# A small GpSimd memset behind each V gather, and a wait for it

## The reference, cut to what matters

```python
def expert_block(args):          # ht: 128 tokens x 1024, it: 128 x 128 indices, gt: 128 x 128 gates
    ht, it, gt = args
    ue = jnp.take(u, it, axis=0)                       # a row of u for each index
    act = jax.nn.gelu(jnp.einsum('tkd,td->tk', ue, ht), approximate=False)
    ve = jnp.take(v, it, axis=0)                       # a row of v for each index
    return jnp.einsum('tk,tkd->td', gt * act, ve)
```

## Time and profile before

| what | value |
|---|---|
| median of 3 runs | 1728.86 us |
| lowest and highest run | 1720.82 and 1728.88 us |
| the profiled execution's own time | 1726.55 us |
| its span, first to last instruction | 1725.3 us |
| granted TensorE clock, mean | 0.959 |
| busy: PE, DVE, ACT, POOL | 1504.8, 1079.1, 661.9, 547.5 us |
| gathers: packets, bytes | 73728, 268.47 MB |

### The profile page before, as it was taken

How to read it: one execution, slowest core, us unless ns; L and a number is a source line. 1 busy time by engine, 2 the same in 40 slices (tenths; PEclk the granted TensorE clock), 3 DMA queues, 4 the chain that set the end, 5 groups by cost and what they waited for, 6 DMA issues and landing times.

```text
span 1725.3 us, 19276 instructions
## 1 busy us (share of the span) xinstructions
PE 1504.8 (87%) x7183; PEld 1083.1 (63%) x7183; DVE 1079.1 (63%) x1970; ACT 661.9 (38%) x1102; POOL 547.5 (32%) x608
## 2 busy tenths in 40 slices
PE   7999999999999999999999888988677666777676
PEld 6888897888788788888899764543232222222222
DVE  5766645686664676675656675647675566666544
ACT  5545534785453555453725231222221121212111
POOL 1000001211000000000100356666666666766664
PEclk9999999999999999999999999999889888998899
DMA  8556454333353455564344889999999999999997
GB/s 282 179 187 195 149 183 158 106 134 105 122 183 111 157 195 195 182 187 156 123 132 164 282 319 352 367 367 367 374 365 375 376 377 373 378 367 357 362 372 294
DMA packets 199943, 431.87 MB, mean 250 GB/s; under 512 B 20774, under 2 KB 114091, under 8 KB 199851
## 3 DMA queue, kind: packets, MB, share of 16 engines
q0 software_dynamic: 73728, 268.47, 40.7%
q1 hardware_dynamic: 123312, 159.66, 28.5%
q10 hardware_dynamic: 2810, 2.52, 0.5%
HBM read 429.55 MB, written 1.05 MB: 250 GB/s over the span
## 4 chain that ended last, share of the span: by engine, by line
PE 52%; DVE 12%; issue 10%; POOL 9%; ACT 7%; another core or an unknown queue 5%; DMA 3%; DVEq 2%; ACTq 0%; POOLq 0%
PE ps L431 51%; POOL GS L2696 5%; POOL RAW L2696 3%; DVE WL L1786 3%; ACT WH L1260 2%; DMA RAW<-in_peer_u_dram,AR 2%; DVE GS L2535 1%; POOL AR L2696 1%; ACT AR L1744 1%; DVE RAW L2535 1%; DMA GS<-in_peer_v_dram,AR 1%; DVE XN L1823 1%; DVE H L1828 0%; DVEq L2367 0%
## 5 line engine op out<-in xcount | busy, mean ns | idle before, releaser
L431 PE MATMUL ps<-XX,WH 128*128 128x256 f32 (+1 forms) x1872 | 467.5, 330 | 9.7 <-DVE XX L1842 5.1
L1786 DVE TENSOR_TENSOR WL<-RAW,WH 128x2048 fp32r<-128x2048 f32 x135 | 309.7, 2294 | 187.0 <-ACT WH L1260 186.4
L431 PE MATMUL ps<-XX,WL 128*128 128x256 f32 x1288 | 364.3, 283 | 0.0
L431 PE MATMUL ps<-GS,AR 128*128 128x512 f32 x526 | 270.5, 650 | 107.2 <-issue 48.7
L431 PEld LDWEIGHTS ps<-XX,WH 128*128 128x128 f32 x1872 | 316.7, 192 | 47.2 <-issue 7.4
L1260 ACT ACTIVATE WH<-RAW 128x2048 fp32r<-128x2048 f32 x129 | 247.1, 1915 | 95.3 <-PE ps L431 95.1
L431 PEld LDWEIGHTS ps<-GS,AR 128*128 128x128 f32 x526 | 103.1, 206 | 263.9 <-issue 203.6
L431 PEld LDWEIGHTS ps<-XX,WL 128*128 128x128 f32 x1288 | 246.8, 192 | 0.7
L2586 POOL TENSOR_TENSOR small<-small 128x1 f32<-128x1 f32 x28 | 15.4, 557 | 683.0 <-DVE small L1818 365.3
L431 PE MATMUL ps<-RAW,AR 128*128 128x512 f32 x348 | 174.1, 632 | 47.2 <-issue 32.4
L2535 DVE CUSTOM_DVE_ANT_0 GS<-GS,ps 128x1024 f32<-128x1024 f32 x135 | 163.0, 1217 | 59.1 <-DMA GS<-in_peer_u_dram,AR 47.1
(11 more groups left out here) (377 smaller groups left out, 1872.9 us busy)
## 6 DMA issues: line engine op xcount, KB each, us to landing
RAW<-in_ffn_w_gu_dram SPq DMA_DIRECT2D x44, 1024.0 KB, 5.1
RAW<-in_w_in_dram SPq DMA_DIRECT2D x39, 1024.0 KB, 5.2
RAW<-in_ffn_w_down_dram SPq DMA_DIRECT2D x22, 1024.0 KB, 5.0
RAW<-in_w_out_dram SPq DMA_DIRECT2D x12, 1024.0 KB, 5.0
RAW<-in_xa_wkv_dram SPq DMA_DIRECT2D x8, 1024.0 KB, 5.4
RAW<-in_xa_wq_dram SPq DMA_DIRECT2D x4, 1024.0 KB, 5.3
RAW<-in_xa_wo_dram SPq DMA_DIRECT2D x4, 1024.0 KB, 5.1
RAW<-in_w_peer_q_dram SPq DMA_DIRECT2D x4, 1024.0 KB, 5.3
```

The lines of the kernel that those rows point to most:

```text
L431: return nc.tensor.matmul(out_, lhsT, rhs, start=start, stop=stop, skip_group_check=True)
L1786: nc.vector.tensor_tensor(conv(1, k, kt), v, conv(0, k, kt).bitcast(F32), ALU.subtract).then_inc(S["lo"], 1)
```

## The change

A tile of 16 columns is added at the end of the memory arena. From item 9 on, GpSimd sets it to zero behind each item's `v` gather and waits until that memset has signalled its end, before it goes on to the next item. No engine reads the tile. `j` runs from 9 to 263, which makes 255 memsets and waits.

```diff
@@ -291,6 +291,7 @@
     diag = [a2(P) for _ in range(8)]
+    pace = a2(16)
     spots = [GS[:, i, :] for i in range(12)]
@@ -2695,6 +2696,9 @@
                     nc.gpsimd.indirect_dma_start(spots[s], None, table, bass.IndirectOffsetOnAxis(
                         un[m % 3]["idx"][:, row % 16:row % 16 + 1], 0)).then_inc(S["gather%d" % s], 16)
+                if j > LAG:
+                    nc.gpsimd.memset(pace, 0.0).then_inc(S["paced"], 1)
+                    pool.wait_ge(S["paced"], j - LAG)
                 if j == LAG - 1:
```

## The result

The changed kernel takes 1729.9 us (median of 15 runs, 1726.4 to 1734.6), the kernel before 1723.1 us in the same series (15 runs). The ratio is 1.0040 with a 95% interval of 1.0027 to 1.0054: 6.8 us more. I had forecast 20 us more. It lies nearest to the rival that I called hidden.

A forecast was written before the change was run, and what follows sets the result against it. In the gather stage GpSimd's issuing with nearly saturated DMA engines alternates with 83 us of stops. 254 x 0.15 = 38 us added, half showing (19) plus 1, gave +20 us on 1726.55: 1747 us, range 1710 to 1812.

The forecast's parts named there:

- hidden: Rival for GpSimd's stops in the gather stage: 83 us of stops take up all 38 us added; 1727 us, chance 0.24.
- What bounds the stage: Gather stage, 732 us: GpSimd issues as fast as it can with DMA engines just keeping up, alternating with stops, 83 us.
- The price: GpSimd time for one memset and its wait: 0.15 us, bounds 0.06 and 0.65; 254 times makes 38 us.
- the 0.77 us: Time in the earlier trace from DVE's indices being ready to the gather's start; gave the upper price, 0.65 us a memset.
- What of it shows: GpSimd's stops in the gather stage cover between none and all of 38 us; the middle, 19 us, plus 1, shows.
- one turn of the ring: GpSimd reaches a slot again after 23 gathers, 1.7 us later; each of 28 stops could shrink by that, 48 us.
- The 1 us for the eight last rows: At the last eight `v` gathers no stop is left to cover the memsets, so 1 us more shows.
- Its second form: Variant of the hidden rival: the memset holds nothing up because the gather's own preparation runs beside it; same 1727 us.
- The broken flow: Rival: the next gather can't be prepared during the wait and begins 0.77 us after the signal; 1809 us or more, chance 0.24.
- The faster rival: Stops at each unit vanish as gathers land sooner; gains once stops fall under 45 us; 1707 us, chance 0.12.
- The estimate by it: Two dispatch hops of about 156 ns on top of each GpSimd memset, 79 us in all; the prediction didn't add them.
- What would have shown it: Signs in the changed trace: 1.40 us from `v` to `u`, about 65 us of "remote" and PE waits, DMA share about 0.94.

The follow-up runs named there:

- e7 to e10: Against the kernel before: memset and wait in the first half only 1.0028, second half only 1.0003; half the bytes per gather 0.9924, the same with memset and wait 1.0096.
- e2: Two memsets per item, each waited for, in place of the changed kernel's one; 1795.8 us, ratio 1.0883 to the kernel before.
- e11: Two memsets per item on two tiles with one wait for both, in place of the changed kernel's one memset; 1673.0 us, ratio 1.0145 to the kernel before.
- e6: Kernel before with most v rows multiplied twice on TensorE, plus the memset and its wait; 1900.2 us, against 1899.0 us for the doubled work alone.
- e13: Kernel before with five rows multiplied 17 times on TensorE, plus the memset and its wait; 1703.9 us, against 1697.0 us for the hold-ups alone.
- e1: Changed kernel without the wait right behind each memset (16 tiles in turn, waiting only for the memset sixteen items before); 1650.0 us, ratio 1.0002 to the kernel before.
- c1_before: The kernel before, unedited, run again at a granted clock near 1.00; 1650.2 us, ratio 1.0005.
- c2_after: The changed kernel, unedited, run again at a granted clock near 1.00; 1660.0 us, ratio 1.0063 to the kernel before.

## Why the prediction was wrong

**What bounds the stage.** I had read it as stretches in which GpSimd issues as fast as it can and "the DMA engines just keep up", and I saw PE's cadence of 2.56 us an item against GpSimd's 2.51. Both readings were right, and I drew no sum from them. (A smaller slip: three stops, 6.6 us in all, stood among the gaps that I had put down to the issuing.) The difference of 0.05 us is the DMA engines' rate. A delay of 0.10 us on GpSimd exceeds it by 0.05, so about half of the 26 us is free even where GpSimd never stops. That is what the condition without stops shows, 10.3 us, and what e7 to e10 take apart. In the first series this cover is small, as its stops keep the backlog short: the k-th 0.5 MB landed 5.4 us after the start of its gather before the change and 4.9 after it (medians).

**The price.** This term was too large. I had it between 0.06 and 0.65 us and took 0.15; it is 0.10. The pieces: the gap ahead of the gather came out at 0.27 us, as the release by PE of the earlier trace rows had it (0.26). The memset began at once and took 0.13 us. The 0.04 us that I added for a slower next gather weren't there: it took 0.95. This makes 26 us of the 38. A gap near the upper one, 0.61 us for 0.77, exists: with two waits in a row (e2). I had put the 0.77 us down to a gather with two things to wait for, behind a wait of another kind. That e11, with one wait, is back at 0.27 is in line with it, and no run tests that gather itself.

**What of it shows.** This step failed. I argued that the stops shrink or don't, and took the middle, half. With the right 26 us it would still have made 13, and 1 for the last rows; 6.8 showed, a quarter. I had given the movement of PE's signals with the gathers too much weight. With the five hold-ups, where single stops can be compared, the stops shrink by 20.6 of the 24 us that were added between them, and only the rest moves the signals. With TensorE as the steady bound all of it is hidden (e6). Nor did I limit the delay rightly: it was one turn of the ring, 1.7 us a stop, and it is all that has gathered since the last stop. The 1 us for the eight last rows had the wrong sign, as the part behind the last gather became 3.3 us shorter. For the first series the count fits, 26 us added and 17 taken from the stops, but it is one trace of each kernel, and that its stops shrink as those of e13 do is carried over, not shown.

What made these stops is open. In the expectations I put them down to TensorE's lower clock, from their absence at a clock of 0.997. The order of time in the first trace speaks against it. Of its 29 stops above 1 us behind the 25th gather 20 began while the granted clock stood at 2.4 GHz; in 9 of these it fell to 1.2 GHz during the stop, in 3 within 3 us behind it, in 8 not at all. Only 9 began at 1.2 GHz. In the stop of the earlier trace rows PE's last row ended at 1311.62, GpSimd stood from 1313.27, and the clock fell at 1315.3. So the lower clock mostly did not come first. I had no run in which the clock alone was changed.

**The rivals.** Hidden was nearest: 1727 against 1729.9. Its reason, slots freed at times that don't depend on the gathers, holds for most of the delay at long stops. Its second form, that the gather's preparation runs beside the memset, is what happens without the wait (e1). The broken flow didn't occur with one memset. The faster rival was excluded by its own condition: the stops fell to 60 us by what they are put down to and 76 us by the single gaps behind the first gather, not under 45. It is true that each gather now lands sooner, 4.9 us after its start in place of 5.4 (medians), but nobody was waiting for that.

**The Trainium skill** (GPSIMD Engine Reference, section 3.1) counts two dispatch hops for a GpSimd instruction. The estimate by it was 79 us. The memset without a wait added nothing to the item (e1), so whatever its dispatch takes is hidden; the measurement decides against adding it here.

**What would have shown it.** I had named 1.40 us from `v` to `u`, and it was 1.35; a wait of about 65 us for PE and "remote", and it was 59.6; a DMA share of 0.94, and it stayed at 0.96. The share is a poor sign, though. From c1_before to c2_after it fell only from 1.03 to 1.01 while the gathers came to be issued no faster than they were moved. The GB/s in these windows (411 and 399) and the time to landing (median 15.2 and 6.2 us) tell the two apart.

## What to carry to other kernels

Where one engine issues transfers only a little faster than the DMA engines move them, a small delay on it costs only what it exceeds the difference of the two rates by (here 0.10 us less 0.05 an item), and it costs least where a backlog has already been built up, at the end. Compute both rates (issues per us, and bytes per issue over the rate in GB/s) before asking what a delay costs. Look for stops of the issuing engine as well: each one takes up most of the delay gathered since the last, up to its own length. A wait of an engine for its own last instruction can cost more than that instruction: here the memset was free, its wait was the price, and a second wait in a row cost four times as much.

## What the runs showed of the hardware that I had not expected

- The same kernel took 1723 us at a granted clock of 0.959 and 1649 us at 0.997, with no instruction changed; in the stretch from 1100 to 1600 us it started 352 and 397 gathers.
- Gathers of 4 KB rows ran at 411 GB/s over 500 us.
- The gap ahead of a gather is 0.30 us behind another gather, 0.18 behind a memset that isn't waited for, 0.27 behind one that is, and 0.61 if the queue had waited for another one just before. (For the last one see the open point under e11_two_onewait.)
- In the first trace PE's signals came late and in bunches. Ahead of the stop of the earlier trace rows PE's signals came at 1301.46 and 1309.16 and then five from 1316.86 to 1317.10, 0.06 us apart, while PE had ended its last row at 1311.62 and not begun the next. ACT went on with them:

```profile
1301.48 0.40 ACT L1744 ACTIVATE AR<-cst,AR 128x128 f32<-128x128 f32 x1 [4.16 <-PE ps L431]
1309.18 0.40 ACT L1744 ACTIVATE AR<-cst,AR 128x128 f32<-128x128 f32 x1 [7.30 <-PE ps L431]
```

  In the gather stage of that trace two signals of PE in a row lay up to 21.7 us apart (660 of the execution's 698 are on record), in c1_before never more than 6.9. The ends of matmuls are modelled, so PE may in truth have been later than its rows say. Why is open.
